# Attention stage: one context unit behind every four latent units, with output rows of its own

## What is computed

```python
# 8 differential heads, then 8 grouped-query (GQA) heads of 128
def diff_attention(q1, q2, k1, k2, v, lam):
    a1 = softmax(q1 @ k1.T * 64 ** -0.5)      # per head, per block of 128 queries
    a2 = softmax(q2 @ k2.T * 64 ** -0.5)
    return (a1 - lam * a2) @ v
o_d = rmsnorm(diff_attention(...), subln_g) * (1.0 - lam_init)
def gqa_attention(q, k, v):
    return softmax(q @ k.T * 128 ** -0.5) @ v  # 4 query heads share a key head
o = concatenate([o_d, o_g]); x = x + g1 * (o @ w_out)
```

## Time and profile before

| | us |
|---|---|
| median of 3 runs | 2361.98 |
| lowest and highest | 2360.32, 2363.41 |
| the profiled execution's span | 2364.1 |
| PE busy in the span | 2215.2 (94%) |
| DVE, ACT busy | 1512.7 (64%), 1202.5 (51%) |
| first scores of attention | at 671.43 |
| last round's copy ends | at 929.53 |
| first matmul of the output projection | at 935.27 |

### The profile page before, as it was taken

One profiled execution on the slowest core, in us unless ns is written; L12 is line 12 of the kernel. 1 busy time (PEld: TensorE's weight loads), 2 busy tenths in 40 slices (PEclk: granted clock), 3 DMA queues, 4 the chain that ended last, 5 costly groups with the idle time before them and its releaser, 6 DMA issues.

```text
span 2364.1 us, 28774 instructions
## 1 busy us (share of the span) xinstructions
PE 2215.2 (94%) x10944; PEld 1547.9 (65%) x10944; DVE 1512.7 (64%) x1577; ACT 1202.5 (51%) x1255; POOL 241.9 (10%) x97
## 2 busy tenths in 40 slices
PE   5899999999999997999929999999999999999993
PEld 3467777777877775788826666666666666666662
DVE  3242221233556665333268999999999999999994
ACT  4431221122246666112147777777776777777763
POOL 1010000001000000000000111211122222111211
PEclk8999999999999997999959999999999999999997
DMA  9875566654220003222389999999999999999995
GB/s 371 317 238 213 221 235 240 232 196 179 72 92 1 1 1 139 95 72 70 127 318 363 382 383 382 395 390 388 389 388 386 385 382 394 395 386 387 384 376 189
DMA packets 187519, 623.71 MB, mean 264 GB/s; under 512 B 10960, under 2 KB 12496, under 8 KB 156048
## 3 DMA queue, kind: packets, MB, share of 16 engines
q1 hardware_dynamic: 177328, 565.76, 63.0%
q0 software_dynamic: 6112, 35.40, 5.4%
q10 hardware_dynamic: 4000, 21.50, 2.3%
HBM read 593.08 MB, written 29.56 MB: 263 GB/s over the span
## 4 chain that ended last, share of the span: by engine, by line
PE 88%; DMA 5%; DVE 3%; ACT 1%; SPq 1%; issue 1%; POOL 0%; ACTq 0%; POOLq 0%; DVEq 0%
PE ps L560 25%; PE ps L561 24%; PE ps L562 24%; PE ps L809 3%; PE ps L755 3%; PE ps L843 3%; DMA arena<-in_w_mod 2%; PE ps L826 1%; PE ps L830 1%; PE ps L958 1%; DVE mx L1545 1%; DMA xn_d<-arena 1%; SPq L624 1%; PE ps L896 1%; PE ps L786 1%
## 5 line engine op out<-in xcount | busy, mean ns | idle before, releaser
L1748 DVE TENSOR_TENSOR E_w_lo<-arena,E_w_hi 128x2048 fp32r<-128x2048 f32 x384 | 871.2, 2286 | 88.5 <-ACT E_w_hi L1248 79.4
L1248 ACT ACTIVATE E_w_hi<-arena 128x2048 fp32r<-128x2048 f32 x380 | 728.8, 1918 | 277.0 <-PE ps L562 277.0
L560 PE MATMUL ps<-E_w_hi,E_xsT_hi 128*80 128x512 f32 x1024 | 404.6, 395 | 2.3 <-DVE E_xsT_lo L1741 2.3
L561 PE MATMUL ps<-E_w_hi,E_xsT_lo 128*80 128x512 f32 x1024 | 403.1, 394 | 0.0
L562 PE MATMUL ps<-E_w_lo,E_xsT_hi 128*80 128x512 f32 x1024 | 400.2, 391 | 0.0
L1528 DVE TENSOR_TENSOR B_w_lo<-arena,B_w_hi 128x1024 fp32r<-128x1024 f32 x72 | 87.6, 1224 | 369.3 <-ACT B_w_hi L1076 369.0
L560 PE MATMUL ps<-B_w_hi,B_x_hi 128*128 128x512 f32 x720 | 290.5, 403 | 1.6 <-DVE B_x_lo L1532 1.1
L561 PE MATMUL ps<-B_w_hi,B_x_lo 128*128 128x512 f32 x720 | 282.2, 392 | 0.0
L562 PE MATMUL ps<-B_w_lo,B_x_hi 128*128 128x512 f32 x720 | 281.7, 391 | 0.0
L1076 ACT ACTIVATE B_w_hi<-arena 128x1024 fp32r<-128x1024 f32 x72 | 75.6, 1058 | 338.9 <-DMA arena<-in_w_in 293.0
L1360 POOL DMA_INDIRECT acc_d<-arena,idxC x16 | 148.9, 9309 | 765.1 <-DVE arena L1792 765.1
(11 more groups left out here) (202 smaller groups left out, 2548.2 us busy)
## 6 DMA issues: line engine op xcount, KB each, us to landing
arena<-in_w_expert_gate SPq DMA_DIRECT2D x128, 1024.0 KB, 12.9
arena<-in_w_expert_up SPq DMA_DIRECT2D x128, 1024.0 KB, 12.5
arena<-in_w_expert_down SPq DMA_DIRECT2D x128, 1024.0 KB, 15.2
arena<-in_w_mod SPq DMA_DIRECT2D x64, 1024.0 KB, 6.4
arena<-in_w_in SPq DMA_DIRECT2D x36, 1024.0 KB, 5.0
arena<-in_w_mod SPq DMA_DIRECT2D x64, 512.0 KB, 9.7
arena<-in_w_out SPq DMA_DIRECT2D x16, 1024.0 KB, 5.3
acc_d<-arena POOLq DMA_DIRECT2D x1, 5120.0 KB, 30.2
```

The lines of the kernel that those rows point to most:

```text
L560: eng.matmul(out, x_hi, w_hi, start=start, stop=False)
L561: eng.matmul(out, x_lo, w_hi, start=False, stop=False)
L1248: act.activation(split_e(j)[0][:, :], at(slot_e(j), D), ACT.Copy).then_inc(xw_hi, 1)
L1748: dve.tensor_tensor(w_lo[:, :], at(slot_e(j), D), w_hi[:, :].bitcast(F32), ALU.subtract).then_inc(xw_lo, 1)
```

## The change

The units are no longer numbered tile by tile. A list ATT names tile and head of every turn: after each fourth latent unit comes one context unit, in the order of its heads. So the turns of latent heads 3, 7, 11 and 15 of each latent tile are followed by one context unit; context heads 0 to 7 (diff) fall into latent tiles 0 and 1, heads 8 to 15 (GQA) into tiles 2 and 3, and the last turn is context head 15. Context rows go to `orow_ctx`, in words that the projection's x_hi left free, so they don't share `orow`. The output rounds are placed by a table: the context tile's rounds 0 to 2 at (2, 6), (2, 8) and (3, 5), round 2 of tile 3 at (3, 15), and after the last unit round 3 of tile 3 and round 3 of the context tile. The work of the steps is the same; the lists of PE, DVE and ACT are permuted, those of SP and POOL are not.

```diff
+CTX_EVERY = TL
+ATT = []
+for _i in range(TL * HEADS):
+    ATT.append((_i // HEADS, _i % HEADS))
+    if _i % CTX_EVERY == CTX_EVERY - 1:
+        ATT.append((TL, _i // CTX_EVERY))
+AT_UNIT = {x: u for u, x in enumerate(ATT)}
+NORM_ORDER = [t for t, j in ATT if j == DH - 1]
+OT_AT = {(t, 11 + 2 * r): (t, r) for t in range(TL) for r in range(2)}
+OT_AT.update({(t + 1, 1 + 2 * r): (t, 2 + r) for t in range(TL - 1) for r in range(2)})
+OT_AT.update({(2, 6): (TL, 0), (2, 8): (TL, 1), (3, 5): (TL, 2), (3, 15): (TL - 1, 2)})
+OT_END = [(TL - 1, 3), (TL, 3)]
...
-        orow = at(W0 + 3840, HEADS, HD)
+        orow_lat = at(W0 + 3840, HEADS, HD)
+        orow_ctx = at(H0 + (NT + 1) * VW, HEADS, HD)
...
         def unit(u):
-            t, j = u // HEADS, u % HEADS
+            t, j = ATT[u]
...
             def take_out(u):
-                t, j = u // HEADS, u % HEADS
+                t, j = ATT[u]
+                orow = rows_of(t)
                 if not is_diff(u):
-                    if t > 0 and j % 4 == 0:
+                    if 0 < t < TL and j % 4 == 0:
                         dve.wait_ge(ot_done, OT_LIST.index((t - 1, j // 4)) + 1)
...
                 if j == DH:
-                    dve.wait_ge(or_ready, t + 1)
+                    dve.wait_ge(or_ready, NORM_ORDER.index(t) + 1)
```

More of the change, by code:

```diff
@@ L84 @@
 UNITS = NT * HEADS
+CTX_EVERY = TL
[5 more added lines that the diff above has]
+AT_UNIT = {x: u for u, x in enumerate(ATT)}
+assert len(AT_UNIT) == UNITS
+NORM_ORDER = [t for t, j in ATT if j == DH - 1]
[3 more added lines that the diff above has]
+OT_END = [(TL - 1, 3), (TL, 3)]
 def group_of(n):
@@ L292, in build @@
         PT = at(W0 + 2560, 2, TOK)
-        orow = at(W0 + 3840, HEADS, HD)
+        orow_lat = at(W0 + 3840, HEADS, HD)
+        orow_ctx = at(H0 + (NT + 1) * VW, HEADS, HD)
+        assert (NT + 1) * VW + HEADS * HD <= KC * TOK
         osq = at(W0 + 5888, DH * HD)
@@ L575, in is_diff, with tails_to, rows_of @@
         def is_diff(u):
-            return u % HEADS < DH
-        def diff_before(u):
-            return (u // HEADS) * DH + min(u % HEADS, DH)
-        def ot_round(u):
-            t, j = u // HEADS, u % HEADS
[L585 to L591, removed]
+            return ATT[u][1] < DH
+        def tails_to(u):
+            return len([x for x in ATT[:u + 1] if x[0] < TL and x[1] < DH])
+        def rows_of(t):
+            return orow_lat if t < TL else orow_ctx
+        def ot_round(u):
+            return OT_AT.get(ATT[u])
+        OT_LIST = [ot_round(u) for u in range(UNITS) if ot_round(u)] + OT_END
+        assert len(set(OT_LIST)) == 4 * NT
         def S_ps(u):
@@ L805, in scores @@
                     if n == 3:
-                        pe.wait_ge(tail_scored, diff_before(u + 1))
+                        pe.wait_ge(tail_scored, tails_to(u))
                     rows = slice(0, HD) if comps == 1 else slice(DQ * c, DQ * (c + 1))
@@ L848, in out_transposes @@
                 if r < 2:
-                    pe.wait_ge(onorm_ready, t + 1)
+                    pe.wait_ge(onorm_ready, NORM_ORDER.index(t) + 1)
                 else:
-                    pe.wait_ge(o_taken, HEADS * t + DH + 4 * (r - 2) + 4)
+                    pe.wait_ge(o_taken, AT_UNIT[(t, 4 * r + 3)] + 1)
                 for h in range(4):
-                    mm = pe.transpose(bank(6)[:, HD * h:HD * (h + 1)], orow[:, 4 * r + h, :], ident[:, :])
+                    mm = pe.transpose(bank(6)[:, HD * h:HD * (h + 1)], rows_of(t)[:, 4 * r + h, :], ident[:, :])
                 mm.then_inc(ot_done, 1)
@@ L871, in _ @@
             values(UNITS - 1)
-            out_transposes(NT - 1, 2)
+            out_transposes(*OT_END[0])
             pe.wait_ge(ot_taken, len(OT_LIST) - 1)
-            out_transposes(NT - 1, 3)
+            out_transposes(*OT_END[1])
             pe.wait_ge(ot_taken, len(OT_LIST))
@@ L1137, in _ @@
                     act.wait_ge(av_done, u)
-                    act.activation(orow[:, (u - 1) % HEADS, :], bank(7)[:, P:2 * P], ACT.Copy,
+                    t, j = ATT[u - 1]
+                    act.activation(rows_of(t)[:, j, :], bank(7)[:, P:2 * P], ACT.Copy,
                                    scale=rsum[:, (u - 1) % 4, 0:1]).then_inc(o_taken, 1)
@@ L1147, in _ @@
                 ins.then_inc(pt_copied, 1)
-            take_ot(NT - 1, 2)
-            take_ot(NT - 1, 3)
+            take_ot(*OT_END[0])
+            take_ot(*OT_END[1])
             act.wait_ge(scored, UNITS)
```

1 line of the change is left out of this document (removed).

## The result

| | before | after |
|---|---|---|
| median of 7 runs each, us | 2362.68 | 2371.01 |
| lowest and highest | 2360.17, 2364.42 | 2367.88, 2371.89 |
| span of the profiled execution | 2364.1 | 2370.1 |
| first scores to last round's copy | 258.10 | 263.34 |
| last round's copy to the end of the span | 1434.6 | 1433.5 |

The change makes the kernel slower, by 0.3%: ratio of the times 1.0031, 95% interval 1.002 to 1.0041. The profiled execution's own time was 2371.89 us, 1.8 more than its span and 0.9 above the median.

The account below looks back on a forecast made before the run. Attention is bound by a loop (values, take, fifth transpose, copies, values), not PE's work. Inserted units and rounds 36.2 plus end 4.5 against 33.1 lose 7.6 us; clock falls add 3.4: 2361.98 + 11.0 = 2373.0 us, range 2365 to 2379.

Parts of the forecast that it names:

- diff c between diff units: Context diff unit between latent diff units, 2 places: take waits behind maxima and exponentials, +1.85 us each.
- behind head 7, diff c / GQA c: Context unit behind latent head 7, 4 places: transposes wait for the squares' reciprocal, +2.3 us diff, +3.3 GQA.
- behind head 15, diff c / GQA c: Context unit behind head 15, 3 places within: latent diff maxima precede its take, +1.15 us diff, +2.65 GQA.
- squares of the context tile: DVE's squares fall behind context head 7, into tile 2's diff units: of 2.6 us some +1.6 remain.
- four rounds: Four output rounds from in or behind the context stage now stand between latent units: 0.45 us each, +1.8.
- last latent values to last copy: End of attention: transpose, copy, values, then two rounds in sequence at full clock, about 4.5 us.
- falls of the clock: PE's clock falls behind head 7 in tiles 2 and 3, at 1.7 us each: +3.4 us.
- the short scores: A context unit's short scores two turns earlier give back 0.37 us in a diff stretch.
- all seven holes: PE waits of 1.8 us or more: every head 7, context squares, two GQA takes; falls at all, 12 us.
- rival 3: Attention's loops lengthen as forecast but the clock holds: 2369.6 us, chance 0.30.
- rivals 3 to 5: Loops lengthen: clock holds, 2369.6 (chance 0.30); two falls, 2373.0 (0.38); falls at most holes, 2378 (0.15).
- Rival 1: Inserted units vanish into PE's gaps, costing only PE's work, 0.75 us diff, 0.53 GQA: about 2345, chance 0.05.

Follow-up runs that it names:

- take_first: Changed kernel with DVE's takes of context GQA outputs, and the norm with them, ahead of the maxima: 2363.73 us, ratio 1.0001.
- act_first: Changed kernel with ACT's take of a context diff output ahead of the exponentials: 2376.81 us, ratio 1.0051.
- the third's: Changed kernel unaltered, compared a third time with the kernel before, in more rounds: 2369.07 us, ratio 1.0022.
- halves_tf2: Kernel before, context heads 0-7 grouped behind head 11 of tile 3, DVE's context GQA takes ahead of the maxima, norm behind them: 2357.94 us, ratio 0.9977.
- take_first2: Changed kernel with DVE's takes of context GQA outputs ahead of the maxima, the norm left behind them: 2363.11 us, ratio 0.9995.
- no_squares: Old order with own context output rows, without the context tile's squares and their sums on DVE: 2359.96 us, ratio 0.9985.
- halves_tf: Kernel before, context heads 0-7 grouped behind head 11 of tile 3, DVE's context GQA takes and the norm ahead of the maxima: 2362.0 us, ratio 0.9997.

## Why the prediction was right, and where not

The forecast was 2373.0 us, 2365 to 2379, slower. Measured 2371.01, inside the range. Step by step (c is the context unit), each as latent values against latent values of the earlier trace rows:

| step | predicted | measured |
|---|---|---|
| diff c between diff units | +1.85 | +1.52 |
| GQA c between diff units | +2.85 | +2.67 |
| diff c between GQA units | +1.5 | +1.42 |
| GQA c between GQA units | +2.1 | +2.11 |
| behind head 7, diff c / GQA c | +2.3 / +3.3 | +2.3 / +3.05 |
| behind head 15, diff c / GQA c | +1.15 / +2.65 | +0.97 / +2.35 |
| squares of the context tile | +1.6 | +1.65 |
| four rounds | +1.8 | +1.6 |
| last latent values to last copy | 4.5 | 4.79 |
| attention, net | +7.6 | +5.24 |
| falls of the clock | +3.4 | 0, 0 and +3.2 in three traces |

**What bounds: right.** The loop values, take, fifth transpose, copies, values is what an inserted unit lengthens, and the order of two in-order lists sets by how much: take_first gives back 4.7 us by moving seven short instructions and the norm, act_first loses 5.1 by moving the other eight. For a diff context unit, whose take stands behind ACT's exponentials, the price is read from the timeline; no run removed it. PE's own work didn't change.

**The sum of the loops: too large by 2.4 us.** No single term is off by more than 0.33, but nearly all err to the same side. I added handing-over times between steps that in the trace overlap: in the first timeline the exponentials start 1.85 after the values where I had 1.96, and the take 1.54 after them where I had 1.67, so that it starts at 3.39 and not 3.6. The rest of that term's 0.33 is the short scores, which gave back 0.46 us and not 0.37. Such differences over fifteen inserted units make most of the 2.6 between the sum's 36.2 and the 33.6 measured from unit to unit; the end took 0.3 back. Apart from the sum, the context stage's excess was read as one hole of 2.13 us with the norm behind it; the norm has a wait of its own, 1.47 us at 914.89.

**The clock: right size, wrong certainty, and partly wrong places.** I put falls behind head 7 of tiles 2 and 3 because PE has least work there. In three traces of the same kernel there are none, none and two, the two behind heads 7 and 15 of tile 2. I gave all seven holes 1.8 us or more. Three measured 1.83 (behind head 7 of tiles 0, 1 and 3), and no trace of this kernel has a fall there; the others were 1.57 us at the squares, 1.39 behind head 7 of tile 2, and 1.20 twice. The term was priced well (1.7 against 1.6, with 3.4 us at half and not 4) and counted wrongly: 3.2 / 3 = 1.1 us on the mean of the traces. With it attention is 6.4 us longer than before on the mean (264.4 against 258.06), and the three ratios, 1.0022 to 1.0031, are 5.2 to 7.3 us. That accounts for the time within the intervals. How often unprofiled executions have a fall wasn't seen. In the words of the prediction, by its first two traces rival 3 (2369.6) was right: attention was 263.3 and 263.4 us long, under the 265 given as a sign, and the clock stayed at 1.00 behind head 7 of tiles 2 and 3. By the third trace (266.5, with two falls) the forecast was, one of the two at another place. The median lies between the two. That it came within 2.0 us of the forecast is in part luck: attention, loops and falls together, was put at 11.0 us and is 6.4 longer on the mean of the traces, while this comparison's medians stand 8.3 us apart and the third's 5.4.

One reading was too general: that it takes over 4 us of dense work for the clock to come back. From the output projection's first matmul to full clock it was 4.4 us in the trace that I read, and 3.0, 6.2 and 3.8 in the three of the changed kernel. And the chances don't add up: rivals 3 to 5 hold 0.83, slower was given 0.81.

**Rival 1 and its rule: not borne out.** Each inserted unit cost 1.0 to 3.1 us, not 0.5 to 0.75, and PE's weight loads went from 73% to 65% of the time (43.48 of 66.46). The Trainium skill (Perfetto Trace Analysis, Optimization Strategy) says that interleaving stretches with different bounds may improve performance. Here it depended on the grain: halves_tf2 interleaves once and is 5.3 us faster than the kernel before, the changed kernel interleaves fifteen times and is 5 to 8 us slower.

**Outside attention: right.** From the last copy to the end 1433.4 to 1436.1 us in all fourteen traces, the changed kernel's three (1433.5, 1436.1, 1434.3) among the others.

## What to carry to other kernels

Before short units are spread among long ones, write down for each in-order list what stands between a short unit's result and the instruction that frees its buffer: that distance, paid once per insertion, is the price, and it does not shrink with the unit. Where they are inserted, insert them together (1.4 us each in a group of eight here, 1.6 in a group of four), and cut the group so that the small tile's one long step falls under other work; grouping without that only reached the time before. Try a short take ahead of the long steps on one engine at a time and with nothing carried along: it won 4.7 us on the engine that waited 0.3 us for its input, lost 5.1 on the one that waited 1.4 with other work ready, and in the sparse context stage cost 3.9 where it brought a 1.2 us step along.

## What the runs showed of the hardware

- In three executions the changed kernel's list met the same six waits of PE of 1.20 to 1.83 us between 800 and 910 us; the clock fell behind two of them (1.39 and 1.20 us) in one execution and behind none in the others. These two falls, the one in take_first2 (from 808) and the one in act_first (from 845) stood at half for 3.4 us each, and cost 1.2 to 1.6. So a fall among busy turns was cheap here, and a single trace did not show whether a list is prone to it. The Trainium skill (TensorE: Matmul & The Clock Gate, What's actually happening) says that the point at which the clock comes up under sustained matmuls varies from run to run. The traces agree on that: the output projection of the changed kernel was at half for its first 3.0, 6.2 and 3.8 us.
- In the sparse context stage a fall lasted longer: behind waits of 1.61, 1.68 and 2.13 us (no_squares, halves_tf, and the old order in its three traces) the clock stayed at half for 23.9 to 27.3 us, into the output projection. Of the 4.1 us between halves_tf and halves_tf2, 3.1 came behind the wait itself. Behind a wait of 0.68 us (halves_tf2, at 911.18) it stayed at full in the same stage, with PE busy 3.42 us of the 5 from 910 on. Whether the hole or the sparse work around it decides wasn't separated, nor how much of the 3.1 us is the clock's.
